# The 32 sample tokens leave the dense expert stages of a hybrid decoder step, their expert rows fetched by index

## The reference

```
q = x @ w_q                                 # 8 heads x 2 halves of 128
s1, s2 = q[..., :128] @ keys1.T, q[..., 128:] @ keys2.T      # 128 scores per half
v1, i1 = top_k(s1, 16); v2, i2 = top_k(s2, 16)
sc, pos = top_k(v1[:, None] + v2[None, :], 16)               # per head and token
idx = (i1 * 128 + i2) at pos;  gate = softmax(sc)
act = gelu(u_tab[idx] . x, exact) * gate                     # 128 experts per token
out = sum over the 128 of act * v_tab[idx]
```

## Time and profile before

| | us |
|---|---|
| median of 3 runs (lowest, highest) | 2356.89 (2355.27, 2357.67) |
| profiled execution | 2357.76 |
| its span, first to last instruction | 2356.0 |
| PE busy | 2158.3 (92%) |
| DVE busy | 1722.0 (73%) |
| ACT busy | 1263.2 (54%) |
| POOL busy | 579.2 (25%) |

### The profile page before, as it was taken

How to read it: one execution, slowest core, us unless ns; L and a number is a source line. 1 busy time by engine, 2 the same in 40 slices (tenths; PEclk the granted TensorE clock), 3 DMA queues, 4 the chain that set the end, 5 groups by cost and what they waited for, 6 DMA issues and landing times.

```text
span 2356.0 us, 53148 instructions
## 1 busy us (share of the span) xinstructions
PE 2158.3 (92%) x18562; PEld 1732.3 (74%) x18562; DVE 1722.0 (73%) x3454; ACT 1263.2 (54%) x2428; POOL 579.2 (25%) x451
## 2 busy tenths in 40 slices
PE   2477989989999999999988898998999999999998
PEld 1355867767888788888866655776788887888886
DVE  8899569966999855555544545999499996555555
ACT  2321468854444455555578454886444444555554
POOL 3996047941000000000037401786200000000000
PEclk7698799999999999999999857999999999999999
DMA  2000334545554455656554204465554545556653
GB/s 79 5 0 1 109 112 146 175 136 164 157 156 152 146 178 177 176 177 180 175 202 147 77 7 155 127 179 158 153 153 151 160 153 156 176 178 176 178 177 117
DMA packets 88953, 328.94 MB, mean 140 GB/s; under 512 B 10785, under 2 KB 10785, under 8 KB 88481
## 3 DMA queue, kind: packets, MB, share of 16 engines
q1 hardware_dynamic: 88272, 318.36, 44.7%
q0 software_dynamic: 592, 9.47, 1.0%
HBM read 321.60 MB, written 6.19 MB: 139 GB/s over the span
## 4 chain that ended last, share of the span: by engine, by line
PE 40%; issue 32%; DVE 21%; POOL 5%; ACT 1%; DVEq 0%; DMA 0%; SPq 0%; POOLq 0%; ACTq 0%
PE ps L282 11%; PE ps L284 11%; PE ps L283 11%; POOL wsp L232 2%; DVE big L800 2%; PE ps L1311 1%; DVE big L789 1%; PE ps L1867 1%; DVE big L1121 1%; DVE big L1130 1%; DVE big L1124 1%; PE ps L888 1%; DVE big L1117 1%; DVE big L1127 1%; DVE big L1149 1%
## 5 line engine op out<-in xcount | busy, mean ns | idle before, releaser
L221 ACT ACTIVATE wsp<-ring 128x512 f16<-128x512 f32 x1200 | 752.5, 629 | 802.0 <-PE ps L284 791.0
L282 PE MATMUL ps<-hs,wsp 128*128 128x288 f16 x2752 | 799.3, 290 | 48.4 <-DVE hs L307 17.6
L283 PE MATMUL ps<-hs,wsp 128*128 128x288 f16 x2752 | 799.2, 290 | 0.0
L284 PE MATMUL ps<-hs,wsp 128*128 128x288 f16 x2752 | 798.6, 290 | 0.0
L234 DVE SCALAR_TENSOR_TENSOR wsp<-ring,wsp 128x512 f16<-128x512 f32 x648 | 446.6, 692 | 406.5 <-ACT wsp L221 406.2
L283 PE MATMUL ps<-hT,wsp 128*128 128x288 f16 (+2 forms) x2560 | 641.0, 263 | 0.0
L282 PE MATMUL ps<-hT,wsp 128*128 128x288 f16 (+2 forms) x2560 | 619.7, 263 | 6.7 <-DVE hT L1451 6.7
L284 PE MATMUL ps<-hT,wsp 128*128 128x288 f16 (+2 forms) x2560 | 619.2, 263 | 0.0
L232 POOL TENSOR_TENSOR wsp<-ring,wsp 128x512 f16<-128x512 f32 x272 | 350.0, 1311 | 187.3 <-ACT wsp L221 186.5
L282 PEld LDWEIGHTS ps<-hs,wsp 128*128 128x128 f16 x2752 | 272.3, 99 | 135.7 <-DVE hs L307 25.4
L284 PEld LDWEIGHTS ps<-hs,wsp 128*128 128x128 f16 x2752 | 273.3, 99 | 73.0
(11 more groups left out here) (251 smaller groups left out, 2167.2 us busy)
## 6 DMA issues: line engine op xcount, KB each, us to landing
ring<-in_v SPq DMA_DIRECT2D x256, 512.0 KB, 3.6
ring<-in_ub SPq DMA_DIRECT2D x184, 512.0 KB, 3.7
ring<-in_ua SPq DMA_DIRECT2D x72, 512.0 KB, 3.7
ring<-in_wq SPq DMA_DIRECT2D x32, 512.0 KB, 3.6
ring<-in_win SPq DMA_DIRECT2D x32, 512.0 KB, 3.8
ring<-in_glu SPq DMA_DIRECT2D x16, 512.0 KB, 3.7
big<-in_hgs POOLq DMA_DIRECT2D x1, 4096.0 KB, 13.6
ring<-in_wout SPq DMA_DIRECT2D x8, 512.0 KB, 4.3
```

The costliest lines, as they stand in the source:

```text
L221: nc.scalar.activation(wsp[:, k % 2, 0, cols], ring[:, k, cols], ACT.Copy, scale=scale).then_inc(hi_ready, 1)
L282: nc.tensor.matmul(out, w_hi, hi, start=start, stop=False, **kw)
L283: nc.tensor.matmul(out, w_hi, lo, start=False, stop=False, **kw)
L284: return nc.tensor.matmul(out, w_lo, hi, start=False, stop=stop, **kw)
```

## The change

The dense stages ua, ub, G and V take 256 tokens (TP) instead of 288. ua has 28 blocks instead of 36; ub has 4 plain blocks and then G with 96 blocks in 8 bodies of 12 blocks and 4 groups. The query stage keeps all 288 tokens. The samples' scores go to other places: 4 heads x 32 tokens lie on the 128 partitions, so that what was a third tile of 32 partitions and 8 heads is one of 128 partitions and 2 heads. It is searched in two small rounds, and its pairs come first.

Their 128 experts a token make 32 slots on the 128 partitions. POOL fetches one slot's 128 rows of u (4 KB each) by index into one of three buffers; 32 fetches for u, then 32 for v. VectorE makes the dot product of a slot's rows with x in the first 64 blocks of V, one every two blocks; ACT takes the 32 gelus; VectorE multiplies by the gates and adds up the weighted rows of v in blocks 73 to 119, two in three blocks. Before the last four blocks TensorE adds the four head groups and transposes, in eight matmuls. The first three fetches stand in POOL's order ahead of the ones, the others behind. x is spread over the partitions in the query stage: a copy, eight transposes after its first block, a copy.

ACT's exponentials stand after 20 blocks of ua (before, after all 36); TensorE's transposes after 24 (before, after ua and four blocks of ub). V's eight chunks of 256 columns fill four banks.

```diff
-UA, UB = 36, 60
+UA = 28
+QH = PH // 4; SLOTS = QH * TK; BUFS = 3              # 2, 32, 3
+        TAIL = NK * TP
+        xrep = big[:, TAIL:TAIL + D]
+        rows = [big[:, TAIL + D * (1 + k):TAIL + D * (2 + k)] for k in range(BUFS)]
...
-        G0 = 5
-        TRIPS, PER = 3, 6
-        SPOTS = [0, 2, 4, 6, 8, 10]
+        G0 = 1
+        TRIPS, PER = 3, 4
+        SPOTS = [0, 3, 6, 9]
...
+            def turn_x():
+                pe.wait_ge(pxd, L + 1)
+                for c in range(KC):
+                    mm = nc.tensor.transpose(ps[:, 2 + c // 4, (c % 4) * P:(c % 4 + 1) * P],
+                                             rows[0][:, c * P:(c + 1) * P], ident[:, :])
...
-                for j, (t0, w) in enumerate(TILES):
-                    for n, (f, m) in enumerate(((0, 0), (1, 0), (0, 1))):
-                        mm = nc.tensor.matmul(ps[0:w, k % 2, j * NK:(j + 1) * NK], qsp[k % 2][:, f, t0:t0 + w],
-                                              ksp[:, m, k % 2, :], start=(n == 0), stop=(n == 2))
+                out = ps[TS * (h % 4):TS * (h % 4 + 1), 2 + h // 4, f * NK:(f + 1) * NK]
+                for n, (a, m) in enumerate(passes):
+                    nc.tensor.matmul(out, qsp[k % 2][:, a, TP:T], ksp[:, m, f, :], start=(n == 0), stop=(n == 2))
+                for j in range(2):
+                    for n, (a, m) in enumerate(passes):
+                        mm = nc.tensor.matmul(ps[:, k % 2, j * NK:(j + 1) * NK], qsp[k % 2][:, a, j * P:(j + 1) * P],
+                                              ksp[:, m, f, :], start=(n == 0), stop=(n == 2))
...
-            for j, (_, w) in enumerate(TILES):           # pairs
+            for j in (2, 0, 1):
+                nh = HEADS[j]                             # [8, 8, 2]
...
+                if j == 2:
+                    for m in range(2):
+                        cnt.add(vv.scalar_tensor_tensor(out=efl[:, m], in0=e12[2][:, m], scalar=float(NK),
+                                                        in1=e12[2][:, 1 - m], op0=ALU.mult, op1=ALU.add))
+                    cnt.wait()
+                    for m, dst in enumerate((row_u, row_v)):
+                        vv.tensor_copy(dst, efl[:, m]).then_inc(pix, 1)
...
+        def fetch_pool(g, L, a, b):
+            if a == 0:
+                g.wait_ge(pix, 2 * L + 2)
+                g.wait_ge(pxc, L + 1)
+                states_out(g, L)
+            for n in range(a, b):
+                if n >= BUFS:
+                    g.wait_ge(taken, 2 * SLOTS * L + n - BUFS + 1)
+                table, idx = (t_in[f"rows{L}"], row_u) if n < SLOTS else \
+                    (t_in[f"v{L}"].rearrange("j i d -> (j i) d"), row_v)
+                nc.gpsimd.indirect_dma_start(rows[n % BUFS], None, table, bass.IndirectOffsetOnAxis(
+                    ap=idx[:, n % SLOTS:n % SLOTS + 1], axis=0)).then_inc(fetched[n % BUFS], 16)
+        def dot_dve(v, L, n):
+            row_here(v, L, n)
+            r = rows[n % BUFS]
+            nc.vector.tensor_tensor_reduce(r, r, xrep, 1.0, 0.0, ALU.mult, ALU.add,
+                                           zs[:, n:n + 1]).then_inc(taken, 1)
+        def sum_dve(v, L, n):
+            row_here(v, L, SLOTS + n)
+            r, w = rows[(SLOTS + n) % BUFS], ws[:, n:n + 1]
...
+                ins = nc.vector.scalar_tensor_tensor(out=acc, in0=r, scalar=w, in1=acc, op0=ALU.mult, op1=ALU.add)
+            ins.then_inc(taken, 1)
+        def sample_out_pe(pe, L):
+            pe.wait_ge(taken, 2 * SLOTS * L + 2 * SLOTS)
+            for c in range(KC):
+                mm = nc.tensor.matmul(ps[:, 4, c * TS:(c + 1) * TS], acc[:, c * P:(c + 1) * P], sel[:, :],
+                                      start=True, stop=True)
...
         def peer_v_dve(v, L):
-            per_block(v, f"v{L}", split_lo, lambda i, k, first: None)
+            sums = {73 + n * 3 // 2: n for n in range(SLOTS)}
+            for b in range(2):
+                split(b)
+            for b in range(NK):
+                if b + 2 < NK:
+                    split(b + 2)
+                if b < 2 * SLOTS:
+                    if b % 2:
+                        dot_dve(v, L, b // 2)
+                elif b == 72:
+                    sample_weights_dve(v, L)
+                if b in sums:
+                    sum_dve(v, L, sums[b])
...
             split_pool(g, "ua0")                          # POOL; the same for layer 1
+            fetch_pool(g, 0, 0, BUFS)
             peer_ones_pool(g, 0)
+            fetch_pool(g, 0, BUFS, 2 * SLOTS)
...
-                peer_u_pe(pe, L, "ua")                    # TensorE
-                peer_u_pe(pe, L, "ub", 0, 1)
+                peer_u_pe(pe, L, "ua", 0, 6)
                 peer_tr_pe(pe, L)
-                peer_u_pe(pe, L, "ub", 1, G0)
+                peer_u_pe(pe, L, "ua", 6, 7)
+                peer_u_pe(pe, L, "ub", 0, G0)
...
-                peer_u_act(act, L, "ua")                  # ACT
+                peer_u_act(act, L, "ua", 0, 5)
                 peer_exp_act(act, L)
+                peer_u_act(act, L, "ua", 5, 7)
...
-                peer_u_dve(v, L, 0, 1)                    # VectorE
                 peer_softmax_dve(v, cnt, L)
-                peer_u_dve(v, L, 1, 2)
                 peer_gates_dve(v, cnt, L)
-                peer_u_dve(v, L, 2, G0)
+                peer_u_dve(v, L, 0, G0)
```

More of the change, by code:

```diff
@@ L65 @@
 N_BLOCKS = dict(SEGMENTS)
-ACC = [[(c, 0, 0, T)] for c in range(6)] + \
-      [[(0, T, 0, 512 - T), (1, T, 512 - T, 2 * T - 512)], [(2, T, 0, 512 - T), (3, T, 512 - T, 2 * T - 512)]]
+QH = PH // 4
+SLOTS = QH * TK
+BUFS = 3
 class Count:
@@ L284, in three_passes, with project @@
             return nc.tensor.matmul(out, w_lo, hi, start=False, stop=stop, **kw)
-        def project(pe, name, wait_bank, after=None, a=0, b=None, inputs=None):
+        def project(pe, name, wait_bank, after=None, a=0, b=None, inputs=None, n=T):
             def post(i, k, first):
@@ L319, in x_chunk @@
             else:
-                eng.wait_ge(pacc[k // 2 - 1], sum(len(ACC[m]) for m in range(c + 1)))
+                eng.wait_ge(pacc[k // 2 - 1], c + 2)
         def square(c):
@@ L1053, in after @@
                     scores(i, k - 1, first)
-                elif not first:
+                elif first:
+                    turn_x()
+                else:
                     scores(i - 1, 3, False)
-            project(pe, f"wq{L}", lambda i, k, first: None if first else pe.wait_ge(pq[L], i * 8 + 2 * k - 6), after,
-                    inputs=(1, 4)[L])
+            for trip in range(4):
+                project(pe, f"wq{L}", lambda i, k, first: None if first else pe.wait_ge(pq[L], i * 8 + 2 * k - 6), after,
+                        trip, trip + 1, inputs=(1, 4)[L])
             scores(3, 3, False)
@@ L1086, in post @@
                     scores_out(i - 1, 3)
-            per_block(act, f"wq{L}", split_hi, post, ahead=2, following=[f"ua{L}"] * 2)
+            for trip in range(4):
+                per_block(act, f"wq{L}", split_hi, post, trip, trip + 1, ahead=2, following=[f"ua{L}"] * 2)
             scores_out(3, 3)
@@ L1114, in peer_topk_dve @@
                 v.wait_ge(pss[L], b + 1)
-                for j, (_, w) in enumerate(TILES):
[L1116 to L1131, removed]
+                best([(score[:, b, j * NK:(j + 1) * NK], val[j][:, f, h], idu[j][:, f, h], rest[j][:, :])
+                      for j in range(2)])
+                if h % 4 == 3 and f:
+                    v.wait_ge(pst, 2 * L + h // 4 + 1)
+                    best([(score_s[:, h // 4, n], val[2][:, n, h // 4], idu[2][:, n, h // 4], rest[n][:, :])
+                          for n in range(2)])
         def peer_pairs_dve(v, cnt, L):
@@ L1222, in peer_exp_act @@
             act.wait_ge(psh[L], 3)
-            for j, (_, w) in enumerate(TILES):
-                nc.scalar.activation(gate[0:w, j], gate[0:w, j], ACT.Exp).then_inc(pex[L], 1)
+            for j in (2, 0, 1):
+                nc.scalar.activation(gate[j], gate[j], ACT.Exp).then_inc(pex[L], 1)
         def peer_tr_pe(pe, L):
@@ L1405, in peer_ug_dve @@
             v.wait_ge(pge[L], GA)
-            g_bodies(v, body, 1)
+            for d in range(BODIES):
+                body(d, d == 0, d == BODIES - 1)
             v.wait_ge(pmul[L], GROUPS)
```

249 lines of the change are left out of this document (164 added, 85 removed).

## The result

| | before | after |
|---|---|---|
| median of the runs, us | 2356.08 (2355.12 to 2357.67) | 2297.20 (2296.79 to 2301.08) |
| span of the profiled execution, us | 2356.0 | 2295.0 |

The ratio is 0.9753, 95% interval 0.9736 to 0.977: 59 us faster. The forecast was 2293.

A forecast was written before the change was run, and what follows sets the result against it. The prediction took TensorE to bound V, with TensorE and VectorE level in G. Per layer 8.4 (U) - 40.5 (V) = -32.1 us, both -64: 2357.8 - 64 = 2293.6, or 2293 against the median; range 2218 to 2354.

The forecast's parts named there:

- V: Expert stretch V: blocks paid by TensorE's columns fall from 2.955 to 2.627 us, giving 40.5 us a layer.
- The sample's matmuls: Ahead of V's last four blocks: eight float32 matmuls of 32 columns add 1.5 us on TensorE.
- The 6 us that V loses at its start: Start of V in layer 0: the 6 us lost there before the change were to stay.
- Dots, sums and fetches: In V: dots and sums hidden on VectorE at about 1.2 us each, fetches landing in 6 to 8 us, also hidden.
- U's start: Before G: TensorE pauses some 25 us ahead of the transposes; G's first body then waits for POOL's ones until 513.6.
- The small tile: Pairs at U's start: cost goes by free elements, at least 8.6 us, taken as 11 with its row numbers.
- The two wide tiles: Pairs at U's start: each takes 34.4 us on VectorE, ending at 439.4 and 473.8.
- the three gathers: POOL ahead of the ones: issuing three gathers takes 6 us, bounds 0 and 15.
- The 1.5 us for turning x: Query stage: eight float32 transposes after its first block add 1.5 us on TensorE's path, to 392.1.
- G: 96 blocks of U: VectorE's order makes TensorE wait every third block; cycle 9.8 us, U ends at 822.2.
- Rival 1: In G: TensorE alone sets the cycle, 8.74 us, total 2229 us; chance 0.16 with what lies between.
- The sum: Per layer, U's cost of 8.4 us less V's 40.5 gives -32.1 us; both layers -64.

## Why the prediction was right, and where not

**V** was right: the splits of two blocks stand 2.62 us apart at the median (2.627 predicted). It gave 43.3 us in layer 0, not 40.5. The sample's matmuls took 1.87 us where 1.5 was said. The 6 us that V loses at its start did not stay: 828.50 to 834.54 less a block leaves 3.4.

**Dots, sums and fetches** were hidden, as forecast. A dot takes 1.22 us and 0.08 for its accumulator, a sum 1.28. Gathers land in 5.3 us (rows of u) and 7.7 us (rows of v), where 6 to 8 were taken. By the Trainium skill's half rate ("Vector Engine (DVE) Microarchitecture Reference", section 7) a sum would have taken an estimated 2.2 us. The measured 1.28 us with two float32 operands in SBUF doesn't bear that out.

**U's start** came out at 513.57 against 513.6, by two errors that cancel. The small tile took 19.6 us (393.93 to 413.5) instead of 11: its cost does not go by free elements alone while POOL runs. The sign of it was there in the earlier trace rows: the same cast takes 0.29 us in one tile and 1.05 in the next. The two wide tiles took 63.2 us instead of 68.8 (34.6 and, with POOL idle for half of it, 28.6), so the softmax came at 476.7 instead of 473.8. Against that the three gathers held POOL 4.0 us, not 6. The 1.5 us for turning x can't be seen: the query stage was to end at 392.1 and ended at 389.79, but this point differs by some 4 us among the kernels here that share the stage.

**G** had the right mechanism; its cycle was taken a little too short. The cycle is 9.98 us and not 9.8. The chain of VectorE is as predicted, 642.45 to 649.60 = 7.15 us; the rest, 649.60 to 652.43, is 2.83 us where 2.613 and a wake were taken: ScalarE starts some 0.2 us after a block's 2.62. Over 30 cycles that is 5.4 us, most of the 6.3 by which U ended late (828.5 against 822.2). Rival 1's 2229 us, a cycle set by TensorE alone, is what the changed order of VectorE then gave: 2226.9.

**The sum** was -32.1 us a layer; layer 0 gave -28.7 (14.6 - 43.3). Two misses of opposite sign, G's +6.3 and V's -2.8, make the difference, so the time of 2297 against 2293 is closer than its terms. U and V of layer 1 gave -29.5, and the stretches between and behind them some 3 us: in all the spans differ by 61 us.

**Open**: why V's start lost less than before, and how the rate of the gathers divides between POOL and the queue, were not tried.

## What to carry to other kernels

When a change takes columns from TensorE, look at the stage's loop of waits before counting them: a stage in which no engine is full can still be bound by the order of one engine's instructions. Here one moved instruction was worth 70 us, more than the change itself. Work hidden behind another engine should be priced with the slack left over: VectorE had 12% of its time left in the stretch with the sums, and sums of twice the length took back the whole gain.

## What was not expected of the hardware

- VectorE's casts and two-input operations beside a busy POOL: 1.11 against 0.20 us for the same 128x64 cast, 2.48 against 0.54 us for five additions, 2.06 against 1.23 us for a product of 128x2048 float16. A reduction of that size takes 2.29 us in both.
- The gather of 128 rows of 4 KB costs POOL 1.14 us (rows of u) and 1.44 us (rows of v) and lands in 5.3 and 7.7 us, with the ring loading beside it; with two on their way instead of three, 4.7 and 6.2 us.
- 291 GB/s instead of 200 in V made no block longer (2.66 and 2.67 us), though a ring load took 4.9 instead of 3.5 us.
